# Query and key columns reordered so that the two attention maps of a head lie on the two halves of the partitions

## The reference

```python
def qk_heads(t, g):
    bn, tn, _ = t.shape
    return rmsnorm(t.reshape(bn, tn, 2, B_HEADS, B_QK_DIM), g)

def diff_attention(q, k, v, lam):
    s = jnp.einsum('bqahd,bkahd->bahqk', q, k).astype(jnp.float32) * (B_QK_DIM ** -0.5)
    p = jax.nn.softmax(s, axis=-1)
    a = (p[:, 0] - lam * p[:, 1]).astype(v.dtype)
    return jnp.einsum('bhqk,bkhe->bqhe', a, v)
```

## Time and profile before

| what | value |
|---|---|
| median of 3 runs | 3279.34 us |
| profiled execution, its own time | 3280.78 us |
| its span | 3279.0 us |
| TensorE busy | 2960.3 us, 90% |
| GpSimd busy | 2178.3 us, 66% |
| ScalarE busy | 1458.4 us, 44% |
| VectorE busy | 1369.4 us, 42% |
| mean granted clock of TensorE | 0.95 |
| attention loops of the second block (starts of the first and last scores) | 1519 to 1656, 2194 to 2355, 2815 to 2973 us |

### The profile page before, as it was taken

How to read it: one execution, slowest core, us unless ns; L and a number is a source line. 1 busy time by engine, 2 the same in 40 slices (tenths; PEclk the granted TensorE clock), 3 DMA queues, 4 the chain that set the end, 5 groups by cost and what they waited for, 6 DMA issues and landing times.

```text
span 3279.0 us, 50143 instructions
## 1 busy us (share of the span) xinstructions
PE 2960.3 (90%) x21088; PEld 2698.8 (82%) x21088; DVE 1369.4 (42%) x1915; ACT 1458.4 (44%) x1906; POOL 2178.3 (66%) x912
## 2 busy tenths in 40 slices
PE   7998989989989799688998987889989987999898
PEld 7877869978779599577888986768889976788898
DVE  2455331133544311424673343346744335467333
ACT  4654544446544544334444443334444443444443
POOL 6667778876677788555566874545467864556586
PEclk9999989999999899889999998889999988999999
DMA  6444445554444555433343543333344543333354
GB/s 211 147 154 174 157 165 187 182 185 142 155 167 155 179 174 183 141 129 128 129 147 137 181 167 137 110 106 113 110 154 155 181 174 103 116 115 130 129 191 144
DMA packets 136513, 495.27 MB, mean 151 GB/s; under 512 B 15072, under 2 KB 17760, under 8 KB 135136
## 3 DMA queue, kind: packets, MB, share of 16 engines
q1 hardware_dynamic: 131904, 480.53, 42.3%
q10 hardware_dynamic: 4384, 11.54, 1.0%
HBM read 488.86 MB, written 3.15 MB: 150 GB/s over the span
## 4 chain that ended last, share of the span: by engine, by line
PE 75%; DVE 12%; ACT 6%; issue 2%; DVEq 2%; POOL 1%; ACTq 1%; DMA 1%; SPq 0%
PE lin L420 16%; PE lin L421 15%; PE lin L422 15%; PE aux L420 4%; PE aux L422 4%; PE aux L421 4%; DVE Z L1752 3%; DVE k_st L1740 3%; ACT whi L893 2%; PE aux L793 2%; PE aux L490 2%; PE lin L446 2%; PE lin L448 2%; PE lin L447 2%; POOL wlo L399 1%
## 5 line engine op out<-in xcount | busy, mean ns | idle before, releaser
L399 POOL TENSOR_TENSOR wlo<-raw,whi 128x1024 fp32r<-128x1024 f32 x908 | 2178.1, 2414 | 1085.5 <-ACT whi L893 1084.9
L893 ACT ACTIVATE whi<-raw 128x1024 fp32r<-128x1024 f32 x908 | 949.3, 1057 | 1170.4 <-PE lin L422 884.4
L420 PE MATMUL lin<-in_hi,whi 128*128 128x256 f32 x3968 | 1170.9, 295 | 113.9 <-issue 33.3
L421 PE MATMUL lin<-in_lo,whi 128*128 128x256 f32 x3968 | 1145.9, 289 | 0.0
L422 PE MATMUL lin<-in_hi,wlo 128*128 128x256 f32 x3968 | 1144.7, 288 | 0.0
L420 PEld LDWEIGHTS lin<-in_hi,whi 128*128 128x128 f32 x3968 | 785.9, 198 | 157.0 <-issue 88.9
L421 PEld LDWEIGHTS lin<-in_lo,whi 128*128 128x128 f32 x3968 | 786.1, 198 | 4.6 <-issue 3.8
L422 PEld LDWEIGHTS lin<-in_hi,wlo 128*128 128x128 f32 x3968 | 784.9, 198 | 0.0
L420 PE MATMUL aux<-br_hi,whi 128*128 128x256 f32 x880 | 249.4, 283 | 7.5 <-DVE br_lo L1294 7.5
L421 PE MATMUL aux<-br_lo,whi 128*128 128x256 f32 x880 | 249.1, 283 | 0.0
L422 PE MATMUL aux<-br_hi,wlo 128*128 128x256 f32 x880 | 249.0, 283 | 0.0
(11 more groups left out here) (231 smaller groups left out, 3864.2 us busy)
## 6 DMA issues: line engine op xcount, KB each, us to landing
raw<-in_wstream SPq DMA_DIRECT2D x908, 512.0 KB, 3.2
Z<-in_rel ACTq DMA_DIRECT2D x2, 1536.0 KB, 8.0
Z<-in_mem_t ACTq DMA_DIRECT2D x2, 1024.0 KB, 7.2
kv_store<-Z ACTq DMA_DIRECT2D x2, 1024.0 KB, 6.9
Z<-kv_store ACTq DMA_DIRECT2D x2, 1024.0 KB, 12.7
x<-in_x_t SPq DMA_DIRECT2D x1, 1024.0 KB, 4.8
Z<-in_ctx_t SPq DMA_DIRECT2D x1, 1024.0 KB, 7.8
out_x<-x SPq DMA_DIRECT2D x1, 1024.0 KB, 3.9
```

Source lines behind the costliest of these rows:

```text
L399: pool.tensor_tensor(wlo[s][:, :], raw[s][:, :], whi[s][:, :].bitcast(F32), ALU.subtract).then_inc(lo_pool, 1)
L420: pe.matmul(out, wh, xh, start=start, stop=False, skip_group_check=True)
L421: pe.matmul(out, wh, xl, start=False, stop=False, skip_group_check=True)
L893: act.activation(whi[s][:, :], raw[s][:, :], ACT.Copy).then_inc(hi_ready, 1)
```

## The change

The query and key columns of `w_in` of the second block are put into the order head, map, element, on the host. A tile of 128 columns then holds the two maps of one head, map 0 on partitions 0 to 63 and map 1 on 64 to 127. The addresses in `diff_scores` and `head_keys` follow.

```diff
+    def by_heads(w):
+        qk = w[:, QK_COL:V_COL].reshape(D, 2, 2, NH, 64).swapaxes(2, 3).reshape(D, V_COL - QK_COL)
+        return np.concatenate([w[:, :QK_COL], qk, w[:, V_COL:]], -1)
+
     def second(l):
-        w_in = v["w_in_2"][l]
+        w_in = by_heads(v["w_in_2"][l])
...
     for c in range(4, 8):
-        chunk(v["w_in_2"][1], c * CH)
+        chunk(by_heads(v["w_in_2"][1]), c * CH)
...
         def head_keys(m, h, kts):
-            r, j = 64 * (h % 2), K2 + 2 * (4 * m + h // 2)
+            r, j = 64 * m, K2 + 2 * h
             return zt(j, 2)[r:r + 64] if kts == 4 else zt(j + 1)[r:r + 64]
...
             def diff_scores(n, kts):
                 h, tt = divmod(n, 2)
-                r = slice(64 * (h % 2), 64 * (h % 2) + 64)
                 for m in range(2):
-                    q = zt(Q2 + 4 * m + h // 2)[r, tt * P:(tt + 1) * P]
+                    q = zt(Q2 + h)[64 * m:64 * m + 64, tt * P:(tt + 1) * P]
                     mm = pe.matmul(aux[:, m, 0:kts * P], q, head_keys(m, h, kts), start=True, stop=True)
                 mm.then_inc(scores_done, 1)
```

## The result

The changed kernel takes 3247.63 us (median of 5 runs, 3246.61 to 3250.72) against 3279.34 of the kernel before. The ratio is 0.9903 with a 95% interval of 0.9891 to 0.9915, so it is about 32 us faster. The forecast was 3265.2 us with a range down to 3261, so the direction was right and the gain was more than twice as large as I had said.

The account below looks back on a forecast made before the run. TensorE's instructions were taken to bound the attention loops; savings of 2.5, 6.0 and 5.6 us in the three loops, together 14.1, from 3279.34 gave 3265.2 us, with an 8-in-10 range of 3261 to 3280.

Parts of the forecast that it names:

- What bounds the kernel: In the three attention loops, TensorE's instructions one after another set the time, except where VectorE's chain is late.
- Overlap in order: Of a step's four score instructions only the middle pair overlaps, saving 0.43 or 0.21 us; chance 0.62, 3265.2 us.
- T: Time of one score matmul instruction: 0.43 us with 512 columns, 0.21 us with 256.
- rival 2: Whole maps overlap in the scores, doubling the saving to 28.2 us, so 3251.1 us; chance 0.05.
- rival 1: Score matmuls of the two halves still run one after another, saving nothing, so 3279.3 us; chance 0.26.
- The count of steps: Steps with scores on the chain: 12 of 16 in the first loop, 13 of 16 in the second and third.
- No new wait arises: In ordinary steps, earlier scores make the probabilities earlier by as much, so TensorE's transposes get no added wait.
- The clock: Half-clock running can shift a little on both sides; allowed 2 us in the range.
- Theory "clock": Forecast for the repeat runs: the 7.6 us saved outside the loops is the chance position of TensorE's half-clock stretches.
- No overlap: Score matmuls on different halves are still taken one after another, at 3279.3 us; chance 0.26.
- the paid change of halves: Going between halves in each step's scores costs 0.19 us, 7.2 us in all, so 3286.5 us; chance 0.07.

Follow-up runs that it names:

- map_then_map: The changed kernel with each score matmul cut into two pieces of half the columns, both of map 0 issued before both of map 1: 3249.87 us, ratio 0.9912.
- map0_twice: The changed kernel with the score matmul of map 0 issued twice in each step, to the same place: 3272.17 us, ratio 0.9981 to the kernel before.
- quarters_alternating: The changed kernel with each score matmul cut into pieces of 128 columns, map 0 and map 1 in turn: 3252.93 us, ratio 0.9920.

## Why the prediction was wrong

**What bounds the kernel** was right: TensorE is on the chain in the loops, and shorter scores shortened the steps one for one. Ordinary steps with 512 columns went from 9.18 to 8.33 us apart, which is the change of the chain's piece.

**The step that failed** is "Overlap in order. I assume that the instructions stay in their order: map 0 first, map 0 second, map 1 first, map 1 second". From it followed 3 T and a saving of T. The runs show 2 T and a saving of 2 T, because each half of the rows can start its own instructions past those that wait for the other. It was my rival 2 in substance, at 3251.1 us, and I gave it 0.05. Even its figure is near by luck: it has too many steps in it (below) and nothing for the 4.7 us outside of the loops. The reason that I gave against it was void: "no instruction of TensorE is seen ahead of an earlier matmul" holds in a trace in which no instruction for the other half ever stood behind, so nothing could have overtaken. I discounted just that for rival 1 and not for rival 2. The Trainium skill's page TensorE: Matmul & The Clock Gate, Part 3, which I had behind it, has two statements here. The Trainium skill says there that matmuls on different row groups start about 4 ns apart; the traces show 6 to 7 ns. The Trainium skill also says there that matmuls start and end strictly in program order; the starts don't agree. In `map_then_map` the first instruction of map 1 starts 0.014 us after the first of map 0 and 0.3 us ahead of the second, and in `map0_twice` the last instruction in the program starts ahead of two others. What keeps to the order there is the semaphore.

**The price T** was right: 0.43 and 0.21 us. The weights were no hindrance: the loads of the two halves start 6 ns apart.

**The count of steps** was right for the first loop, one too high for the second and two too high for the third. In loops 2 and 3 the distances from step 8 to 9, 9 to 10, 11 to 12 and 14 to 15 (from 0) didn't shrink by the saving, and at full clock that from step 0 to 1 didn't either: it takes 7.30 us in the third loop of before and 7.24 in the second loop of the changed kernel. There shorter scores leave the chain, because ScalarE's exponential for `lam`, with the load of its table, and VectorE's two small instructions come just as late as the scores did:

```profile
2184.08 1.28 ACT L1228
2185.38 0.21 ACT small L1228
2185.61 0.16 DVE small L1298
2185.85 0.16 DVE small L1298
2186.09 1.23 DVE small L1820
```

The maximum starts 1.92 us after the first scores started, where it started after 1.99 before:

```profile
2814.92 1.97 PE aux L793 x4
2816.91 1.22 DVE small L1816
```

In the second loop the first scores of before ran at half clock and took 3.76 us; that distance shrank by 1.4 to 1.9 us (9.10 to 7.24, 7.70 and 7.48). So 12, 11 and 11 pieces of 2 T give 5.1 + 9.4 + 9.4 = 23.9 us, and with the first scores of the second loop about 25.5. The loops and their last scores gave 25.0 by the means of the traces, but loop by loop 5.5, 11.6 and 7.9: the second had less half clock than before and the third more. The sum fits better than its parts.

**"No new wait arises"** was not quite right. The first step of a loop has it, as shown above: the first transposes of the second loop of the changed kernel wait 2.5 us for the probabilities, those of the first loop 1.4 us, where before had 1.7 in the third loop alone. Over the whole kernel TensorE's waits for the gate reciprocal rose from 24.0 us in 10 to 30.8 us in 12, and those for the probabilities from 7.2 in 6 to 9.8 in 7. The rows of the list of waits, before:

```profile
PE lin L420 <- DVE Z L1752: 24.0, 10, 3.6
...
PE aux L800 <- DVE probs L1828: 7.2, 6, 1.7
```

and changed:

```profile
PE lin L425 <- DVE Z L1756: 30.8, 12, 4.4
...
PE aux L804 <- DVE probs L1832: 9.8, 7, 2.5
```

The reciprocal's row is that of the steps in which a faster TensorE only waits longer for VectorE's 6.56 us.

**The clock.** I gave it 2 us. Outside of the loops, stretches moved by up to 8.6 us between executions of one kernel. On average over the traces 4.7 us of the gain lie outside of the loops. Theory "clock" would explain them by stretches with less time at half clock, which is not shown; that the changed kernel gets them every time between loops 2 and 3 was seen three times out of three, but `quarters_alternating`, with loops as short, took 461.1 us there. So this part of the gain isn't a property of the change that can be relied on.

**The other rivals.** No overlap is refuted by every trace, and so is the paid change of halves: neither a gap nor a late load stands between the two maps.

## What to carry to other kernels

Here two f32 matmuls over 64 partitions with 512 columns took 1.06 us instead of 1.91 once they lay on different halves of the partitions; arranging that can be free, as an order of columns on the host. Issue them so that few of one half stand in a row (here up to four instructions, that is two f32 matmuls, were harmless, and six were not). Before you count a step's saving, ask at each place what else ends just behind the piece that gets shorter: the first step of each loop gained almost nothing at full clock. When a trace has never put two instructions in a position to overlap, its order says nothing on whether they could.

## What the runs showed of the hardware

- The two halves of TensorE's rows take their instructions past each other, within a short way of the program: an instruction for the free half overtook three that waited for the other (start 14 ns after the first, 7 ns if it is next in the program). With six and eight ahead it started beside the third and fifth, 0.331 and 0.555 us late.
- The end of matmuls is reported in the order of the program: in `map0_twice` the instruction that raises the semaphore started 0.85 us ahead of the last one of the other half, and the semaphore rose 30 to 32 ns after that one's end.
- Loads of weights for the two halves run at the same time: in the changed kernel their starts are 2191.402 and 2191.408, and each still takes 0.19 us.
- An f32 matmul over 64 rows appears as two instructions, and both of map 1 ran beside both of map 0. Four on one half took 1.91 us, two and two on both halves 1.06.
- The time at half clock between the same two points of the program differed by 6.8 us between two kernels with the same work there, and that stretch's time by about 3 us. What share of such differences is the clock's isn't shown.
